# A two-layer transformer at full fp32 accuracy on one Trainium2 core: the residual stream kept tokens by features, three of the weight products with the tokens stationary

## What is computed

```python
h = x
for layer in range(2):
    hn = rms_norm(h, norm_mix[layer])
    mix = even_mixer(hn, w_in, ..., w_out) if layer % 2 == 0 else odd_mixer(hn, w_in, w_out)
    h = h + mix
    hn = rms_norm(h, norm_mlp[layer])
    h = h + square(relu(hn @ w_up[layer])) @ w_down[layer]      # 2048 -> 8192 -> 2048
return rms_norm(h, final_norm)
```

## Time and profile before

| | before |
|---|---|
| median of 3 runs | 2144.68 us (2143.99 to 2145.8) |
| the profiled execution, its own time | 2144.6 us |
| its span | 2142.9 us |
| granted TensorE clock, mean | 0.997 |
| TensorE matmul / weight load busy | 2118.4 us (99%) / 1845.2 us (86%) |
| VectorE / ScalarE / GpSimd busy | 1327.2 (62%) / 1138.2 (53%) / 53.7 us (3%) |
| read from HBM | 386.48 MB, 181 GB/s |

### The profile page before, as it was taken

How to read it: one execution, slowest core, us unless ns; L and a number is a source line. 1 busy time by engine, 2 the same in 40 slices (tenths; PEclk the granted TensorE clock), 3 DMA queues, 4 the chain that set the end, 5 groups by cost and what they waited for, 6 DMA issues and landing times.

```text
span 2142.9 us, 34807 instructions
## 1 busy us (share of the span) xinstructions
PE 2118.4 (99%) x12171; PEld 1845.2 (86%) x12171; DVE 1327.2 (62%) x1875; ACT 1138.2 (53%) x1761; POOL 53.7 (3%) x88
## 2 busy tenths in 40 slices
PE   7999999999999999999999999999999999999998
PEld 6888888888888888888888888888888888888887
DVE  7687776556655655667555554766556556655664
ACT  6578655445544544555444555555445545544554
POOL 5021000000000000000000000000000000000000
PEclk9999999999999999999999999999999999999999
DMA  7454666665666566665655544555666665666553
GB/s 240 146 167 138 190 193 187 188 189 183 194 186 189 185 193 186 186 192 183 193 187 187 182 133 128 181 184 186 194 188 187 190 190 178 196 189 187 183 186 128
DMA packets 387645, 389.68 MB, mean 182 GB/s; under 512 B 12240, under 2 KB 385136, under 8 KB 387568
## 3 DMA queue, kind: packets, MB, share of 16 engines
q1 hardware_dynamic: 386640, 385.98, 58.0%
q0 software_dynamic: 800, 2.65, 0.4%
q10 hardware_dynamic: 128, 0.03, 0.0%
HBM read 386.48 MB, written 2.12 MB: 181 GB/s over the span
## 4 chain that ended last, share of the span: by engine, by line
PE 97%; DVE 1%; ACT 1%; POOL 1%; issue 0%; DMA 0%; ACTq 0%; DVEq 0%; POOLq 0%
PE psum L376 89%; PE psum L403 4%; PE psum L1128 0%; POOL relu_sq L898 0%; PE psum L1154 0%; PE psum L840 0%; PE psum L1170 0%; DVE w_split L355 0%; PE psum L978 0%; DMA mix<-in_rel_bias_dram 0%; PE psum L837 0%; PE psum L1156 0%; PE psum L1172 0%; PE psum L1155 0%; PE psum L1129 0%
## 5 line engine op out<-in xcount | busy, mean ns | idle before, releaser
L355 DVE TENSOR_TENSOR w_split<-raw,w_split 128x1024 fp32r<-128x1024 f32 x728 | 884.9, 1227 | 633.7 <-ACT w_split L348 629.5
L348 ACT ACTIVATE w_split<-raw 128x1024 fp32r<-128x1024 f32 x728 | 760.9, 1057 | 705.7 <-PE psum L376 661.2
L376 PE MATMUL psum<-hg_op,w_split 128*128 128x512 f32 (+1 forms) x6016 | 1062.5, 338 | 2.3 <-DVE hg_op L720 2.3
L376 PEld LDWEIGHTS psum<-hg_op,w_split 128*128 128x128 f32 x6016 | 917.3, 188 | 137.1 <-issue 4.2
L376 PE MATMUL psum<-ff_op,w_split 128*128 128x512 f32 (+1 forms) x5120 | 896.2, 337 | 0.0
L376 PEld LDWEIGHTS psum<-ff_op,w_split 128*128 128x128 f32 x5120 | 778.8, 188 | 113.1
L414 ACT ACTIVATE cross<-psum 128x256 f32<-128x256 f32 x348 | 122.2, 377 | 121.3 <-PE psum L376 121.1
L419 DVE TENSOR_TENSOR total<-psum,cross 128x256 f32<-128x256 f32 x348 | 137.9, 418 | 55.3 <-ACT cross L414 55.2
L480 ACT ACTIVATE relu_sq<-relu_sq 128x256 f32<-128x256 f32 x128 | 52.5, 410 | 82.6 <-DVE relu_sq L487 82.6
L403 PE MATMUL psum<-w_split,hg_op 128*128 128x512 f32 (+1 forms) x512 | 89.6, 337 | 0.0
L490 DVE TENSOR_TENSOR ff_op<-relu_sq,ff_op 128x256 f32 (+1 forms) x128 | 54.5, 426 | 55.4 <-ACT ff_op L481 53.3
(11 more groups left out here) (154 smaller groups left out, 516.2 us busy)
## 6 DMA issues: line engine op xcount, KB each, us to landing
raw<-in_w_up_dram SPq DMA_DIRECT2D x256, 512.0 KB, 3.9
raw<-in_w_down_dram SPq DMA_DIRECT2D x256, 512.0 KB, 3.6
raw<-in_odd_w_in_dram SPq DMA_DIRECT2D x96, 512.0 KB, 3.5
raw<-in_even_w_in_dram SPq DMA_DIRECT2D x56, 512.0 KB, 3.9
raw<-in_even_w_out_dram SPq DMA_DIRECT2D x32, 512.0 KB, 4.5
raw<-in_odd_w_out_dram SPq DMA_DIRECT2D x32, 512.0 KB, 3.6
mix<-in_x_dram SPq DMA_DIRECT2D x4, 512.0 KB, 7.5
mix<-rel_dram POOLq DMA_DIRECT2D x4, 512.0 KB, 5.6
```

The costliest lines, as they stand in the source:

```text
L348: act.activation(w_hi[:, slot], raw[:, rs], ACT.Copy).then_inc(hi_done, 1)
L355: dve.tensor_tensor(w_lo[:, slot], raw[:, rs], w_hi[:, slot].bitcast(F32), ALU.subtract).then_inc(lo_done, 1)
L376: ins = nc.tensor.matmul(o, l, r, start=(k == 0 and n == 0), stop=(k == KT - 1 and n == 1), skip_group_check=True)
```

## The change

`h` is now tokens by features ([128, 2, 2048]). The 44 quads of `even_w_out`, `odd_w_out`, all down quads and v are "wide": the tokens (hi or lo, 128 of them) are stationary, the weights move, 512 columns at a time, and a sub is 256 rows by 512 columns of weights, loaded as such. Per 128 rows and 128 tokens there are three matmuls of 512 columns into one bank. A quad has 96 matmuls of 512 columns, a sub 12. The other 47 quads (up, `even_w_in`, q and k) are as they were.

VectorE adds the PSUM bank straight to `h` (128x512, two per quad); the copy by ScalarE and the sum by VectorE fall away. The squares are taken by ScalarE with a sum along the row (`square_act`), and VectorE brings the sums into the form that `norm` takes (`norm_sum`). The inputs of norms 1, 2 and 3 are transposed on TensorE, 8 transposes at a time (`turn_pe`), four times a norm, into banks 4 to 7, and ScalarE and VectorE write `hg_op` from there. At the start the copy into `h` and GpSimd's sums fall away. At the end the transposes back (7 groups of 4 between matmuls, one behind) fall away: GpSimd and VectorE multiply by the gain, and the output leaves in 8 pieces for 6. Down quads are written out one by one where they were loops.

```diff
-        def pe_sub_tok(pe, Q, s, pos, op, ready, base, first):
...
+        def pe_sub_wide(pe, Q, s, op, ready, base, first, after_wide):
+            slot, pair = s % SPLIT_SLOTS, first % 2
+            pe.wait_ge(lo_done, 8 * Q + s + 1)
...
+            hi, lo = rows_512(w_hi[:, slot]), rows_512(w_lo[:, slot])
             for tb in range(TB):
...
+                acc = psum[:, 2 * pair + tb]
...
+                for kt in range(2):
+                    k = 2 * s + kt
+                    xh, xl = op[:, k, tb * P:(tb + 1) * P], op[:, k, S + tb * P:S + (tb + 1) * P]
+                    nc.tensor.matmul(acc, xh, hi[:, kt], start=(k == 0), stop=False)
+                    nc.tensor.matmul(acc, xh, lo[:, kt], start=False, stop=False)
+                    ins = nc.tensor.matmul(acc, xl, hi[:, kt], start=False, stop=(k == KT - 1))
...
+        def turn_pe(pe, nrm, n, Q):
+
+            pe.wait_ge(bank_free, 4 * Q + 4)
+            if n >= 2:
+                pe.wait_ge(hg_ready, KT * nrm + 4 * (n - 1))
+            for pair in range(2):
+                turn_pair(pe, 4 + 2 * (n % 2) + pair, 4 * n + 2 * pair)
...
+        def residual(which, eng, Q, n, nrm):
+
+            cols = bass.ds(4 * P * n, 4 * P)
+            for tb in range(TB):
+                if which == "dve":
+                    eng.wait_ge(pe_count, after_half(Q, tb))
+                    eng.tensor_tensor(h[:, tb, cols], h[:, tb, cols], psum[:, 2 * (n % 2) + tb], ALU.add).then_inc(bank_free, 2)
+                elif nrm is not None:
+                    eng.wait_ge(bank_free, 4 * Q + 2 * tb + 2)
...
+                    square_act(eng, nrm, n, tb)
...
+        def norm_sum(dve, n):
+
+            dve.wait_ge(sq_done_tok, 8 * (n + 1))
...
+            link("dve", dve, dve.tensor_reduce(sq_tok[:], sq_part[:], AX_X, ALU.add))
+            for tb in range(TB):
+                ins = dve.tensor_scalar(ssq[:, tb * P:(tb + 1) * P], ident[:], sq_tok[:, tb:tb + 1], None, ALU.mult)
+            ins.then_inc(ssq_done, 1)
...
-            pe.wait_ge(h_ready, KT)
+            pe.wait_ge(hg_ready, KT)
             nc.tensor.transpose(psum[:, 5, 0:8 * NL], prow[0:8 * NL, 1], ident[0:8 * NL, 0:8 * NL]).then_inc(par_pe, 1)
...
             with eng.Fori(1, CHUNKS - 1) as c:
-                with eng.Fori(0, 4) as g:
+                up(c, 0, None, True)
+                with eng.Fori(1, 4) as g:
                     up(c, g)
-                with eng.Fori(0, 4) as g:
-                    down(c, g)
...
+                for n in range(4):
+                    down(c, n)
```

More of the change, by code:

```diff
@@ L326, in even_out_tiles, with rows_512, load_quad @@
             return even_out_count(*([("swa", g) for g in range(HA // 4)] + [("lru", m) for m in range(NL // 2)])[:n // 2])
-        def load_quad(eng, Q, w, row, col, places=range(8)):
+        def rows_512(v):
+            return v.rearrange("p (t a) n -> p t (a n)", a=2)
+        def load_quad(eng, Q, w, row, col, wide, places=range(8)):
             for s in places:
@@ L335, in load_quad @@
                     eng.wait_ge(lo_done, 8 * Q + s - RAW_SLOTS + 1)
+                if wide:
+                    src = w[bass.ds(row + s * 2 * P, 2 * P), bass.ds(col, 2 * GC)]
+                    eng.dma_start(rows_512(raw[:, slot]), src.rearrange("(t p) n -> p t n", p=P)).then_inc(raw_in[slot], 16)
+                    continue
                 g, kq = divmod(order(Q)[s], 4)
@@ L474, in hidden, with turn_pair @@
-        def hidden(which, eng, Q, g, U, n0):
+        def turn_pe(pe, nrm, n, Q):
[4 more added lines that the diff above has]
+                turn_pair(pe, 4 + 2 * (n % 2) + pair, 4 * n + 2 * pair)
+        def turn_pair(pe, bank, k):
+            for j in range(2):
+                for tb in range(TB):
+                    ins = nc.tensor.transpose(psum[:, bank, j * S + tb * P:j * S + (tb + 1) * P],
+                                              h[:, tb, (k + j) * P:(k + j + 1) * P], ident[:])
+            ins.then_inc(tr_pe, 1)
@@ new lines, in turn_hook, with hook, square_act @@
+        def turn_hook(nrm, n, Q):
+            first = 0 if n == 3 else 1
+            def hook(which, eng, s):
+                if which == "pe":
+                    if s == first:
+                        turn_pe(eng, nrm, n, Q)
+                elif which in ("act", "dve") and s == first + 1:
+                    for pair in range(2):
+                        (turn_act if which == "act" else turn_dve)(eng, nrm, 4 + 2 * (n % 2) + pair, 4 * n + 2 * pair)
+            return hook
+        def square_act(act, nrm, n, tb):
+            if nrm + n + tb:
+                act.wait_ge(sq_done_tok, 8 * nrm + 2 * n + tb)
+            act.activation(sq_out, h[:, tb, 4 * P * n:4 * P * (n + 1)], ACT.Square,
+                           accum_out=sq_part[:, tb, n:n + 1]).then_inc(sq_done_tok, 1)
@@ L476, in hidden @@
+        def hidden(which, eng, Q, W, g, U, n0):
             if which == "act":
@@ L561, in hook @@
             def hook(which, eng, s):
+                if which == "dve" and s == place - 2:
+                    norm_sum(eng, n)
                 if s == place - (which == "pe"):
@@ L1259, in mlp, with down @@
-            up(0, 0, norm_hook(nrm))
+                         lambda which, eng, grp: hidden(which, eng, Q, W0 + 4 * c + g, grp, U0 + 4 * c + g, 4 * g),
+                         hook, after_wide)
+            def down(c, n, prep=None, hook=None, until=8):
+                Q = Q0 + 8 * c + 4 + n
+                run_quad_wide(which, eng, Q, wd, D * c, 512 * n, ff_op, ff_ready, A0 + KT * c,
+                              lambda which, eng: residual(which, eng, Q, n, prep), n, hook, n > 0, until)
```

459 lines of the change are left out of this document (198 added, 261 removed).

## The result

The changed kernel takes 2126.56 us (2126.01 to 2127.58, 4 runs) against 2144.37 us of the kernel before, measured beside it; the ratio is 0.9916, its 95% interval 0.9899 to 0.9933. The forecast was 2154.0 us and slower, with a range of 2147 to 2159. It was wrong in sign. What came true is the rival with a large fixed price per matmul, which the prediction had put at 2130.0 us and a chance of 0.08.

A forecast was written before the change was run, and what follows sets the result against it. The prediction took TensorE, busy 99% of the span, as the bound. It summed 2144.6 + 4.0 (matmuls) + 7.4 (transposes) - 1.3 (start) - 0.7 (end) = 2154.0 us, 0.43% slower, range 2147 to 2159.

The forecast's parts named there:

- the rival with a large fixed price per matmul: Wide quads: 14.2 ns per matmul, so fewer matmuls give -20.0 us and 2130.0 us in all; chance 0.08.
- the price of a single matmul: TensorE's matmuls: 0.233 us for 512 columns, 0.115 for 256, read from single starts; cost goes by columns.
- the term +4.0 us for the matmuls: The 44 wide quads: 0.08 to 0.11 us more each, 3.5 to 4.7 us in all, taken as +4.0.
- The small price: Rival for wide quads: 0.0025 us saved per matmul fewer, term -3.5 us, 2146.5 us in all; chance 0.08.
- stationary operand: All quads: which operand is stationary is worth nothing by itself; 22.29 us a quad either way.
- the transposes: On TensorE between matmuls: 96 new, 28 gone, 0.11 us each, without cover; together +7.4 us.
- no new wait: Quads with transposes: additions, splits and the writing of `hg_op` end before TensorE needs them; cost 0.
- The start: Before the first quads: first sub about 0.8 us earlier, norm's matmul no longer waits; gain 1.3 us, bounds 0 and 2.5.
- The end: Behind the last matmul: first output DMA after 4.2 us instead of 4.9; gain 0.7 us, bounds -1 and +2.
- no wait for code: Chunk loop's branch back on TensorE: the main forecast added no time for fetching code.
- the rival of 2159 us: Chunk loop: the longer body makes two branches back wait for code, 2.4 to 8 us, taken as 5; chance 0.11.

The follow-up runs named there:

- e1_halves: The changed kernel with every 512-column matmul of the 44 wide quads as two of 256 columns: 2189.26 us, ratio to before 1.0206.
- e10_narrow256: The changed kernel with the 512-column matmuls of the 47 narrow quads (weights stationary) as two of 256: 2159.65 us, ratio to before 1.0069.
- e2_mixed: The changed kernel with only the middle of the three wide matmuls (x_hi with w_lo) as two of 256 columns: 2150.07 us, ratio to before 1.0023.
- e4_twice: The changed kernel with each of the 96 transposes that feed norms 1 to 3 done twice: 2137.74 us, ratio to before 0.9966.
- e3_grouped: The changed kernel with narrow quads' matmuls grouped by width, 2 to 3 width changes a sub for 8: 2130.70 us, ratio to before 0.9934.
- e6_alternate: The changed kernel with narrow quads' matmuls strictly in turn, 512, 256, where they stood in pairs: 2136.30 us, ratio to before 0.9961.
- e12_phase: The changed kernel with narrow quads in turns of 256, 512, but 512 first in each bank's first row and behind norms: 2138.65 us, ratio to before 0.9972.
- e9_quarters: The changed kernel with every 512-column matmul of the wide quads as four of 128 columns: 3064.11 us, a single run.

## Why the prediction was wrong

- **Failed: the price of a single matmul.** The step is "Two 256 cost 0.230: a matmul costs by its columns, and nothing per matmul can be seen", and from it the term +4.0 us for the matmuls. Measured, the term is -23.3. The total of a quad, 22.29 us, was right. What was wrong was to split it with the distances between starts, read to 0.01 us, in a stream of two widths. Alone among its like a 512 costs 0.2267 and a 256 0.120 (e1_halves, e10_narrow256, both forms); mixed, they were read as 0.233 and 0.115 apart, so part of the 256's price shows on the 512. The evidence against the rival ("where this asks 0.121 and 0.228") was this reading; the rival's two numbers are what uniform streams show.
- **The rival that came true** had -20.0 for the matmuls where -23.3 came: it spread the whole excess of 1.81 us over the number (1.81 / 128 is 14.1 ns, it had 14.2). Of that 0.0133 x 128 = 1.71 is the price per matmul and 0.107 goes with the mixing, and a wide quad saves both: 0.427 + 0.107 = 0.53 a quad. That the rival's time came within 3.5 us is so in part luck, as it priced no mixing.
- **The small price and the page.** bf16 quads follow the rule that the prediction cited from the Trainium skill ("TensorE: Matmul & The Clock Gate", Back-to-back issue gap), columns over 2.4 GHz plus 2.5 ns: 0.2158 us for 512. For fp32r the price is 13.3 ns, and no run here follows the rule in fp32r.
- **Right: stationary operand.** e2_mixed gives 22.29 with the tokens stationary too.
- **Right: the transposes.** 0.89 us a group of eight for 0.88, and e4_twice doubles them.
- **Right: no new wait.** No quad with a group is longer by more than its transposes (22.65 or 22.66 us in all nine that hold nothing else), and TensorE's idle time before L453 is nothing. The work taken from VectorE and ScalarE is worth nothing.
- **The start: right in its first step, its total luck.** 12.18 came for "about 12.2", and there is no wait before the norm's matmul. But L782 could go at 27.49, 1.5 us earlier than the 29.0 worked out, and the sub behind it then took 4.41 us where it had 3.06, at the lower clock. The two nearly cancel, and -1.4 stands for -1.3. With the same instructions up to here and both subs at full clock, e4_twice reaches the norm's matmul at 30.32 for 32.11:

```profile
27.42 3.07 PE L394 MATMUL psum<-hg_op,w_split 128*128 128x512 f32 x16
30.32 0.59 PE L604 MATMUL psum<-ssq,ones 128*128 128x256 f32 x2
```

- **The end: right to the first transfer, not behind it.** 3.8 us for 4.2 forecast; but the output took 1.0 us longer to leave, so 0.1 to 0.2 of the 0.7 was gained.
- **Right: no wait for code, though not far off.** The changed kernel's branch takes at most 0.21 us, so the rival of 2159 us did not occur. It does in e1_halves, with 2.93 and 2.48 us for the two branches, 5.4 together, where the rival had 5. The Trainium skill ("Runtime: NRT & Kernel Launch", Instruction fetch mechanics) gives TensorE 128 KiB, 2048 instructions, which agrees with a threshold between 1615 and 2127. The sentence that it puts beside this, a store of 32 KiB alone and so a fetch at every taken branch out of two pages, does not: by its own 16 KiB for 256 instructions, 1360 and 1615 would wait too, and they neither wait nor bring in a packet on the second pass.

## What to carry to other kernels

Where TensorE is full, count matmuls as well as columns: in fp32r a matmul with its own weight load costs its columns at 2.4 GHz plus 13.3 ns at 256 and 512 columns (and 112 ns in all at 128), so the same product in 512-column pieces is cheaper, 0.2267 us for 0.240 in two halves; in bf16 the price is 2.5 ns and the choice hardly matters. Price a shape from the length of a long stretch that holds this shape alone; distances between single starts in a mixed stream shift cost from one shape to its neighbour. Keep a loop's body on TensorE at or below some 1600 instructions, weight loads counted; with 2127 its branch back waited for code. Where one number (a stretch) has to be split over two unknowns, give the rivals of that split the chance that its weakness deserves; here it decided the sign.

## What the runs showed that was not expected

- In fp32r the order of widths matters, and I have no rule for it. Beside the fixed price a quad of 64 and 64 costs 0.11 us in pairs (22.29), 0.19 in fours and eights (22.37), and in strict turns 0.00 or 0.42 (22.19 or 22.61), the two lengths with the same instructions at different places of the program. Neither the number of changes (e3_grouped, e6_alternate) nor an odd or even place (e12_phase) explains it. In bf16 it is 0.00 in pairs. It stays open.
- The kernels with bf16 splits are 6.1% faster than the kernel before and 5.3% than the changed one; the columns are the same, the quads take 20.72 for 21.76 and 20.80 for 22.29. That is at a lower accuracy that this study doesn't weigh. Of the kernels at the accuracy of before, none that was tried beats the changed one.
- The clock at the start. The first sub took 4.43 us before and 2.86 after, but the fifth 3.06 before and 4.41 after. Windows of before, then of after (granted clock third from the end), in fractions of the full 2.4 GHz:

```profile
13.02:17.45 4.43, 4.43 (x16) 3.73 (x17) 4.43 (x5) 4.12 (x9) 3.82 (x7) 0.61 1.11 347
29.41:32.47 3.06, 3.06 (x17) 2.43 (x16) 3.06 (x4) 2.10 (x4) 2.04 (x2) 1.00 0.57 179
```

```profile
12.18:15.04 2.86, 2.86 (x17) 2.48 (x17) 1.85 (x3) 2.77 (x10) 2.51 (x4) 1.00 1.08 361
27.70:32.11 4.41, 4.41 (x17) 3.80 (x17) 1.36 (x2) 1.06 (x1) 0.89 (x3) 0.61 1.07 337
```

  One sub at mostly the lower of the two clock levels (1.2 GHz) costs some 1.5 us in either kernel; in the changed one it has moved from the first sub, behind 2.33 us of idle time, to the fifth, behind 2.17 us. It is not part of what the change was meant to gain, but it moves the start by more than that gain was: with no low sub e4_twice is 1.8 us earlier at the norm's matmul. Why one such gap is followed by the lower clock and the other isn't stays open: the changed kernel's first sub stands behind 1.30 us of idle time and runs at full clock, as does the fifth of e4_twice behind 2.17 us, and in e1_halves the gap of 2.93 us at the first branch leaves the clock full, that of 2.48 at the second does not.
- The wait for code reaches 4.3 to 4.8 us at the branch (e1_halves, e9_quarters), of which the matmuls still queued ahead hide 1.7 to 1.8; with 1615 instructions or fewer nothing of it is seen.
